# Layer norm in two token halves between the last output tiles and the next weight chunks, its root on GpSimd, products pass by pass

## The reference

```python
def layer_norm(x, g, b):
    mu = jnp.mean(x, -1, keepdims=True)
    var = jnp.mean(jnp.square(x - mu), -1, keepdims=True)
    return (x - mu) * lax.rsqrt(var + LN_EPS) * g + b

x = layer_norm(ALPHA * x + 0.5 * swiglu(x, ffn1...), ln1_g, ln1_b)      # D_FF = 2816
proj = x @ w_in                                                        # 1024 -> 5792 columns
y_a = mla_branch(...)          # latent attention, 8 heads; rms_norm of two latents (384 and 256 wide)
y_b = short_conv_branch(...)   # gated causal convolution of width 3
y_c = s5_branch(...)           # grouped state space model, scan over tokens
x = layer_norm(ALPHA * x + (g0 * y_a + g1 * y_b + g2 * y_c) @ w_o, ln2_g, ln2_b)
x = layer_norm(ALPHA * x + 0.5 * swiglu(x, ffn2...), ln3_g, ln3_b)
```

## Time and profile before

| | |
|---|---|
| runs shown, median (lowest to highest) | 2890.27 us (2888.03 to 2891.69) |
| the profiled execution's own time | 2893.35 us |
| its span, first to last instruction | 2890.6 us |
| mean granted clock of PE | 0.972 of full |
| DMA | 229.27 MB, mean 79 GB/s |

### The profile page before, as it was taken

The page is one execution under the profiler, slowest core; times in us unless marked ns, Lnnn a source line. Parts: engine busy times, 40 slices in busy tenths (PEclk is TensorE's granted clock), DMA queues, the critical chain, the costliest instruction groups (busy, mean ns, idle before and its releaser), DMA issues.

```text
span 2890.6 us, 56692 instructions
## 1 busy us (share of the span) xinstructions
PE 2710.9 (94%) x22244; PEld 2628.9 (91%) x22244; DVE 1396.7 (48%) x2020; ACT 845.8 (29%) x1236; POOL 1058.6 (37%) x477
## 2 busy tenths in 40 slices
PE   7999998899999989999889999798999999999996
PEld 7999988888889989999789999798888998999995
DVE  6954154935443662121688641649344436522126
ACT  3222223135532242222242222232245222422223
POOL 4444433312234434444334444233222343344431
PEclk9999999999999999999999999899999999999998
DMA  4323323212223323232223232232122232233322
GB/s 142 95 81 92 88 76 81 70 28 59 57 70 87 99 66 92 86 92 84 70 86 88 87 93 84 64 89 63 41 52 60 73 94 88 74 93 88 88 80 73
DMA packets 458206, 229.27 MB, mean 79 GB/s; under 512 B 38112, under 2 KB 455136, under 8 KB 458048
## 3 DMA queue, kind: packets, MB, share of 16 engines
q1 hardware_dynamic: 452864, 219.98, 27.3%
q10 hardware_dynamic: 5184, 7.14, 0.9%
HBM read 222.83 MB, written 2.10 MB: 78 GB/s over the span
## 4 chain that ended last, share of the span: by engine, by line
issue 51%; PE 25%; POOL 21%; DVE 2%; POOLq 1%; ACT 0%; DMA 0%; SPq 0%; DVEq 0%; ACTq 0%
POOL w_lo L393 21%; PE ps L438 21%; PE ps L454 1%; PE ps L737 1%; PE ps L699 1%; PE ps L716 0%; DVE ln_in L1128 0%; POOLq L392 0%; PE ps L703 0%; DVE stat L1143 0%; PE ps L463 0%; DVE stat L1159 0%; DVE ln_in L1112 0%; DVE stat L1129 0%; POOLq L398 0%
## 5 line engine op out<-in xcount | busy, mean ns | idle before, releaser
L393 POOL TENSOR_TENSOR w_lo<-w_raw,w_hi 128x1024 fp32r<-128x1024 f32 (+3 forms) x472 | 1055.9, 2242 | 1785.5 <-ACT w_hi L825 1785.3
L438 PE MATMUL ps<-x_hi,w_hi 128*128 128x264 f32 x4000 | 827.8, 288 | 20.0 <-DVE ln_in L1193 10.2
L438 PE MATMUL ps<-x_lo,w_hi 128*128 128x264 f32 x4000 | 817.6, 286 | 0.0
L438 PE MATMUL ps<-x_hi,w_lo 128*128 128x264 f32 x4000 | 816.8, 286 | 0.0
L825 ACT ACTIVATE w_hi<-w_raw 128x1024 fp32r<-128x1024 f32 (+3 forms) x475 | 453.8, 959 | 867.3 <-PE ps L438 736.9
L438 PEld LDWEIGHTS ps<-x_hi,w_hi 128*128 128x128 f32 x4000 | 627.1, 189 | 32.3 <-issue 24.3
L438 PEld LDWEIGHTS ps<-x_lo,w_hi 128*128 128x128 f32 x4000 | 622.3, 189 | 0.0
L438 PEld LDWEIGHTS ps<-x_hi,w_lo 128*128 128x128 f32 x4000 | 621.6, 189 | 0.0
L1180 DVE TENSOR_TENSOR hid_rest<-hid_rest,ps 128x528 f32<-128x528 f32 x88 | 61.9, 704 | 564.3 <-PE ps L438 537.4
L438 PE MATMUL ps<-hid_hi,w_hi 128*128 128x264 f32 x1408 | 292.5, 289 | 13.4 <-DVE ln_in L1112 12.5
L438 PE MATMUL ps<-hid_lo,w_hi 128*128 128x264 f32 x1408 | 289.6, 287 | 0.0
(11 more groups left out here) (272 smaller groups left out, 3134.4 us busy)
## 6 DMA issues: line engine op xcount, KB each, us to landing
w_raw<-in_ffn_w_gate SPq DMA_DIRECT2D x91, 512.0 KB, 3.8
w_raw<-in_w_in SPq DMA_DIRECT2D x90, 512.0 KB, 3.9
w_raw<-in_ffn_w_up SPq DMA_DIRECT2D x88, 512.0 KB, 3.8
w_raw<-in_ffn_w_down SPq DMA_DIRECT2D x64, 512.0 KB, 3.9
w_raw<-in_ffn_w_down SPq DMA_DIRECT2D x32, 384.0 KB, 3.4
w_raw<-in_w_o SPq DMA_DIRECT2D x16, 512.0 KB, 3.9
w_raw<-in_conv_w_out SPq DMA_DIRECT2D x16, 256.0 KB, 2.8
w_raw<-in_s_w_out SPq DMA_DIRECT2D x16, 256.0 KB, 3.2
```

The costliest lines, as they stand in the source:

```text
L393: pool.tensor_tensor(w_lo[:, s, 0:n], w_raw[:, c % RAW, 0:n], w_hi[:, s, 0:n].bitcast(f32), ALU.subtract).then_inc(w_split, 1)
L438: ins = nc.tensor.matmul(out[0:m, h], w[:, s, cols], x[:, k0 + k, h * HALF:(h + 1) * HALF], start=first and k == 0 and n == 0, stop=last a ...
```

## The change

Feed-forward parts are 6, 8 and 8 hidden tiles. Of the last part's eight output tiles (and of the eight of `w_o`), the first four are made whole and the last four in halves: all four for the first 264 tokens, then all four for the others, each half in a PSUM bank of its own. The norm is done for each half of the tokens by itself: sums, variance, root, scaling; the first half's tail on DVE and ACT is interleaved with taking the second half's tiles. The next four chunks are rounded and split during it, and their products start with the first half: two chunks tile by tile, the second half's sums, the other two chunks, then the same for the second half. The root is a power of -0.5 on POOL, for the latents of the mixer too; ACT's square roots and DVE's reciprocals go. Provisional mean (now of two tiles) and mean stay in PSUM and are subtracted from there. ACT makes all squares. `product` runs all input tiles of one pass before the next pass, and waits for `w_lo` only ahead of the third. `z` stays from the norm for the next block, and after the mixer is rebuilt in the merge loop. In the mixer, convolution tile 2 is before the q latents. S5 table steps move by one part. The output is stored in 16 pieces instead of 8.

```diff
-PARTS = [(0, 8), (8, 8), (16, 6)]
+PARTS = [(0, 6), (6, 8), (14, 8)]
+WHOLE = KD // 2
+HALF_BANK = {4: 0, 5: 2, 6: 1, 7: 3}
 ...
+            def root(l, which, h):                                   # POOL
+                pool.wait_ge(ln_var, (l * 3 + which) * 2 + (h + 1))
+                pool.tensor_tensor(stat[:, 0, HALVES[h]], stat[:, 0, HALVES[h]],
+                                   minus_half[:].to_broadcast([P, HALF]), ALU.pow).then_inc(ln_root, 1)
+            def norm(l, which, c0):
+                root(l, which, 0)
+                for n in range(SLOTS):
+                    split(l, c0 + n)
+                root(l, which, 1)
 ...
+                for c in range(B_M1 + SLOTS, B_HEAD):
                     split(l, c)
+                    if c == B_CONV + 1:
+                        pool.wait_ge(rms_taken, l + 1)
+                        pool.tensor_tensor(stat[:, 3:5], stat[:, 3:5], minus_half[:].unsqueeze(2).to_broadcast([P, 2, L]),
+                                           ALU.pow).then_inc(rms_root, 1)
 ...
+            def product(out, c, k0, hi, lo, n_tiles, first, last, m=P, at=0, split=None, halves=(0, 1)):
+                for n, (w, x) in enumerate(((w_hi, hi), (w_hi, lo), (w_lo, hi))):
+                    if n == 2 and split is not None:
+                        split_ready(*split)
+                    for k in range(n_tiles):
+                        for h in halves:
+                            ins = nc.tensor.matmul(out[0:m, h], w[:, s, cols], x[:, k0 + k, HALVES[h]], ...)
 ...
+            def first_products(l, c, x0, n):
+                for h in range(2):
+                    for j in range(2):
+                        pe.wait_ge(z_half[1], n * 4 + (4 + 2 * h + j + 1))
+                    by_tiles(l, [pair(0), pair(1)], c, xh, xl, x_ready[h], x0, halves=(h,))
+                    if h == 0:
+                        layer_norm_sums(n, 1)
+                    for j in (2, 3):
+                        rounded(l, c + j)
+                        ins = product(pair(j), c + j, 0, xh, xl, KD, True, True, split=(l, c + j), halves=(h,))
 ...
+            def last_tiles(l, which, c, hi, lo, nk):                 # PE
+                for h in range(2):
+                    for d in range(WHOLE, KD):
+                        ...
+                        for p, (w, x) in enumerate(((w_hi, hi), (w_hi, lo), (w_lo, hi))):
+                            for k in range(nk):
+                                ins = nc.tensor.matmul(ps[:, bank, 0:HALF], w[:, s, k * P:(k + 1) * P], x[:, k, HALVES[h]], ...)
+                        ins.then_inc(half_done if h == 0 else chunk_done, 1)
+                        if h == 1 and d == WHOLE:
+                            layer_norm_sums(n, 0)
 ...
+            def layer_norm(l, which, bd):                            # ACT
+                for d in range(WHOLE):
+                    round_ahead(l, bd + d)
+                for k in range(3):
+                    square(l, which, k)
+                round_ahead(l, bd + WHOLE)
+                square(l, which, 3)
+                for k in range(4, KD):
+                    square(l, which, k, 0)
+                square(l, which, 4, 1)
+                round_ahead(l, bd + 5)
                 for k in range(KD):
+                    norm_tile(l, which, k, 0)
+                    if k in (1, 4, 6):
+                        square(l, which, {1: 5, 4: 6, 6: 7}[k], 1)
+                        round_ahead(l, bd + {1: 6, 4: 7, 6: 8}[k])
+                for k in range(KD):
+                    norm_tile(l, which, k, 1)
 ...
+                def take_half(k, h):                                 # DVE
+                    ins = stt(z[:, k, cols], ps[:, HALF_BANK[k], 0:HALF], scale, z[:, k, cols], MUL, ADD)
+                    follow(ins, z_half[h], n * 4 + (k - 3) + 4 * h)
+                    follow(tt(z[:, k, cols], z[:, k, cols], ps[:, 6 + h, 0:HALF], SUB), ln_dev, n * 12 + (1 + k + 4 * h))
+                    st.done(tt(S[:, cols], S[:, cols], z[:, k, cols], ADD))
 ...
+                def tail(h):
+                    cols = HALVES[h]
+                    mean, var = ps[:, 4 + h, 0:HALF], stat[:, 0, cols]
+                    dve.wait_ge(ln_stat, n * 5 + (5 + 2 * h))
+                    ...                                              # four dependent operations: the variance
+                    st.done(ts(mean, mean, 1.0 / D_MODEL, None, MUL))
+                    dev = lambda k: tt(z[:, k, cols], z[:, k, cols], mean, SUB)
+                    dev(0)
+                    st.done(dev(1))
+                    dve.wait_ge(ln_root, n * 2 + (h + 1))
+                    for k in range(KD + 1):
+                        if k < KD:
+                            tt(z[:, k, cols], z[:, k, cols], var, MUL).then_inc(ln_scaled, 1)
+                        if k + 2 < KD:
+                            st.done(dev(k + 2))
+                        if k:
+                            dve.wait_ge(ln_hi, m * KD + k)
+                            tt(xl[:, k - 1, cols], z[:, k - 1, cols], xhf[:, k - 1, cols], SUB).then_inc(x_ready[h], 1)
+                        if h == 0 and k in (1, 4, 6):
+                            j = {1: 5, 4: 6, 6: 7}[k]
+                            st.done(add_square(j - 1, HALVES[1], j + 4))
+                            take_half(j, 1)
+                        if h == 0 and k == 7:
+                            add_square(KD - 1, HALVES[1], 12).then_inc(ln_sums, 1)
 ...
+                conv_tile(l, 2, st)
                 latent_tiles(l, 0, st)
-                conv_tile(l, 2, st)
+                conv_tile(l, 3, st)
                 latent_tiles(l, 1, st)
-                conv_tile(l, 3, st)
```

More of the change, by code:

```diff
@@ L396, in ffn @@
             def ffn(l, b0):
-                for (f0, nf), at_ in zip(PARTS, PART_AT):
-                    with pool.Fori(0, nf // 2) as i:
+                for part, ((f0, nf), at_) in enumerate(zip(PARTS, PART_AT)):
+                    with pool.Fori(1 if part == 0 else 0, nf // 2) as i:
                         for n in range(4):
@@ new lines, in ffn, with gate @@
+            def ffn(l, b0, w):
+                def gate(part, i, j, ahead=True):
+                    (f0, nf), bu = PARTS[part], b0 + PART_AT[part]
+                    c = bu + 2 * j
+                    if ahead:
+                        round_ahead(l, c, 1, i, nf // 2)
+                    if isinstance(i, int):
+                        act.wait_ge(chunk_done, done_at(l, c + 4 * i))
+                        dst = glf[:, 2 * i + j]
+                    else:
+                        act.wait_ge(chunk_done, done_at(l, c) + i * 4)
+                        dst = glf[:, ds(i * 2 + j, 1)].rearrange("p a t -> p (a t)")
+                    ACTV(two(dst), pair(2 * j), ACT.Silu).then_inc(silu_done, 1)
+                    round_ahead(l, c + 1, 1, i, nf // 2)
+                gate(0, 0, 0, ahead=False)
@@ L953, in _ @@
                         ACTV(two(kvf[:, n - MT - 3]), src).then_inc(m1_taken, 1)
-                act.wait_ge(rms_taken, l + 1)
-                ACTV(stat[:, 3:5], stat[:, 3:5], ACT.Sqrt).then_inc(rms_sd, 1)
                 for n in range(3 * MT):
@@ L1149, in layer_norm @@
-                ins.then_inc(ln_sums, 1)
-                take(KD - 1)
-                dve.wait_ge(ln_stat, n * 3 + 2)
-                st.done(ts(two(stat[:, 0]), pair(2), 1.0 / D_MODEL, None, MUL))
-                st.done(tt(stat[:, 3], stat[:, 0], stat[:, 0], MUL))
-                dve.wait_ge(ln_stat, n * 3 + 3)
-                stt(two(stat[:, 2]), pair(3), 1.0 / D_MODEL, two(stat[:, 3]), MUL, SUB).then_inc(ln_var, 1)
-                for k in range(2):
-                    dev(k)
-                dve.wait_ge(ln_sd, n + 1)
@@ L1159, in layer_norm @@
[L1159 to L1167 removed]
+                dve.wait_ge(ln_stat, n * 5 + 3)
@@ new lines, in layer_norm @@
+                st.done(ts(pair(3), pair(2), 1.0 / (2 * P), None, MUL))
+                st.done(stt(two(S), pair(3), -2.0, two(S), MUL, ADD))
+                for k in range(3):
+                    tt(two(z[:, k]), two(z[:, k]), pair(3), SUB).then_inc(ln_dev, 1)
+                dve.wait_ge(ln_dev, n * 12 + 3)
+                st.done(tt(S, S, z[:, 2], ADD))
+                st.done(add_square(1, square=2))
+                take(3)
+                follow(tt(two(z[:, 3]), two(z[:, 3]), pair(3), SUB), ln_dev, n * 12 + 4)
@@ L1400, in latents_begin @@
                     dve.memset(v[:, 2 * L:2 * L + P].bitcast(f32), 0.0)
-                dve.wait_ge(rms_sd, l + 1)
-                for n in range(2):
-                    ins = nc.vector.reciprocal(stat[:, 3 + n], stat[:, 3 + n])
-                st.done(ins)
+                dve.wait_ge(rms_root, l + 1)
             def latent_tiles(l, n, st):
```

362 lines of the change are left out of this document (182 added, 180 removed).

## The result

The changed kernel takes 3664.95 us (median of 4 runs, 3662.66 to 3667.11), the kernel before on the same chip 2890.98. The ratio is 1.268, 95% interval 1.266 to 1.270: slower by 27%, where 2860 us was forecast. The profiled execution took 3662.66 us, its span 3660.8, the mean granted clock 0.868 (0.972 before).

What follows compares the result with a forecast made beforehand. TensorE, busy 94% of the span, bounds the kernel; only its waits and lower clock can be won. Norms 17.7, mixer 9.4 and start 3 make 30 us off, from the 2890.27 us median to 2860, range 2818 to 2916.

Steps and rivals of the forecast that it cites:

- R is not in the trace: Step pricing POOL's unseen power for 264 columns: 1.7 us from the reciprocal's 6.5 ns a column, range 0.8 to 3.9.
- R: Time of one POOL power of 264 columns in a norm half, taken as 1.7 us; 6.9 us for the latents' 1056.
- rival (c): Slower: power twice on each norm's path and before the mixer's splits; 2886 us at R = 3, 2926 at 5; chance 0.22.
- Norm, walk: Step-by-step norm timing from tile 4's first half product (T = 0): loss 18.5 + R or 17.5 + 2R per norm.
- Splits beside the tail: POOL splits meeting DVE's dense first-half tail in each norm: three charged at 2.0 us each, 6 us.
- Rival (b): POOL splits don't meet DVE in the norms as charged: about 40 us more gained, 2820 us; chance 0.08.
- Mixer: Earlier convolution tile wins 8.5 us and 1.4 of clock, against 5.2 of waits: +4.7 us a layer, +9.4.
- Feed-forward parts, "0": Parts of 6, 8, 8 with S5 tables moved by a part, where DVE has room: 0 us.
- Pass by pass, "0": Products ordered by pass, same matmuls and weight loads, no run of such half passes in the trace: 0 us.
- (a): The power is cheap, R = 0.8: norms 27.3, mixer 2 x 9.9, start 3, 50 us off, 2840 us; chance 0.18.
- (d): No change: R near 3, or norm tiles nearer 1.5 than 1.16 us from ACT-DVE hand-over; 2885 to 2893 us; chance 0.10.
- (e): The power costs 1.5 times the reciprocal's rate, R = 2.6, the mixer's 10.4 us: 2878 us; chance 0.11.

Runs made afterwards that it cites:

- run 3: Changed kernel with only the latents' root back on ACT's Sqrt and DVE's reciprocals, the norms' twelve powers staying on POOL: 3348.0 us, ratio 1.160.
- run 10: Kernel of run 7 with the four POOL splits beside each norm cut to 8 columns, those remainders left out: 2808.9 us, ratio 0.973.
- run 6: Kernel before with convolution tiles ahead of the latents and products pass by pass, whole-tile norms kept: 2849.2 us, ratio 0.987.
- run 7: Kernel of run 1 with the S5 table steps moved from beside the first part's down products, parts still 6, 8, 8: 2841.9 us, ratio 0.984.
- run 4: Kernel before with convolution tile 2 ahead of the query latents and tile 3 ahead of the key/value latents, roots unmoved: 2867.8 us, ratio 0.993.
- run 5: Kernel before with only each product's matmuls reordered pass by pass; waits, halves and parts stay: 2867.8 us, ratio 0.993.
- run 2: Changed kernel with a cheap product of constants in place of every POOL power, so the output is not the reference's: 2855.3 us, ratio 0.988.
- run 1: Changed kernel with all roots back on ACT's Sqrt and DVE's reciprocal, all else as changed: 2864.0 us, ratio 0.992.
- run 12: Kernel of run 1 with powers of several widths and exponents and a product on POOL behind the last output: 264-column powers 42.5 us each, product 0.62 us.
- run 11: Kernel of run 7 with the second to fourth splits beside each norm done by DVE between its tiles, nothing left out: 2824.9 us, ratio 0.978.

## Why the prediction was wrong

**The step that failed** is "R is not in the trace": the value of 1.7 us and the bounds of 0.8 and 3.9. The lower one held as a bound, the upper one was low by a factor of 11. It had scaled DVE's reciprocal, 4.9 times its subtraction, to POOL; on POOL the power is 42.44 / 0.62 = 68 times a product. No row of before showed anything like it, so a factor taken from another engine's dearest operation was no bound, and the range, the chances and the point of 3.3 us up to which the forecast could stand were all drawn inside it. An estimate from the Trainium skill's page "GPSIMD Engine Reference", section 3.1, was 2.6 us by its branch figure, 10 ns a column; the measured 161 ns a column are 16 times that.

**The mechanism was that of rival (c)**, down to its price of "2 us a norm for each us of R": 484 us for twelve powers (run 3). With R = 42.4 its formulas give 17.5 + 2 x 42.4 = 102.3 us for each of five norms and 119.8 for the last, 471 more than before; for the mixer some 167 us of waits a layer less 9.9, 314; start -3: 782 us, 3672. Measured were 3665. That it comes so near is in part luck, since the terms below are off by up to 22 us, in both directions.

**Norm, walk.** Right to some 0.5 us at the marks of the first norm: variance at T = 18.0 (18.1), DVE on its way at 466.8 (466.9), second power at T = 89.4 (variance at 46.5 + R = 88.9), last tile at T = 141.9 (141.6). Splits beside the tail: charged 2.0 us each, measured 33 us in six norms, 5.5 a norm for three (run 10). Rival (b), which had them at nothing, is out. The 264-column operations are 0.35 and 0.46 us apart as taken.

**Halves, net.** With a root of 2.4 us the formulas give the norms 9 and the start 3 us; the expectation of run 6 said 17 and 3. Measured, from run 6 to run 7: 7 us. Right in sign, too small in size. The waits of 7.5 us behind the moved S5 parameters (run 7), which run 6's kernel lacks, are inside this 7; without them it would be some 14, by an estimate.

**Mixer.** The order of convolution tiles was worth about the 2 x 9.9 us (run 4: 20, with the reciprocals still in their place). The wide power was to cost 5.2 us a layer and cost 159 (317 / 2, run 3); it held DVE's second scan, as said, though only for its first half.

**Feed-forward parts, "0": wrong**, +22 us (run 7). The steps were charged against DVE's busy share of 48%, a mean of the span. What decides is one take interval: 0.7 + 5.3 us of DVE against a product that had just become 4.4 us. DVE was busy 37.98 of 40 us in that very stretch of before (run 7's first row), so it had no room to give. The parameters, moved behind the first hidden tile, cost the 7.5 us more of that run's waits.

**Pass by pass, "0": wrong**, -18 us (run 5). Same matmuls and loads, but another order among them has another pitch. That this zero and the last nearly cancel is luck.

**Rivals.** (a) R = 0.8 is nearly run 2 (0.62 us): 2855 measured for 2840. The two wrong zeros, +22 and -18, and some 7 for the parameters account for 11 of the 15 us, if they hold in that kernel as in the others, which was not tried; the rest stays open. (d) and (e) fall with R.

With ACT's Sqrt and DVE's reciprocal in the power's place the change is a gain of 24 us (run 1), and of 44 with the tables moved (run 7). That root takes 3.1 us from the end of the variance to the end of the reciprocal (run 7, 412.94 to 416.02), in part beside other work of DVE.

## What to carry to other kernels

An operation that no row shows has no upper bound from rows of another engine. Where it sits twice on the path, work out the price per us first, as rival (c) did, and then measure the operation alone before the change is built on it; run 12 would have done. An edit charged at nothing because "the engine has room" needs the row of that very stretch and the interval between two instructions that others wait for, not the busy share of the span. Beside a dense DVE stretch, a POOL split of 2.5 us cost DVE 1.8 us on the path (run 10); the same subtraction on DVE itself, 1.2 us, was the cheaper one (run 11).

## What the runs showed of the hardware that was not expected

- POOL's elementwise power takes 160 ns a column plus 0.3 us, for exponents -0.5 and 2.0, for 32 and for 128 partitions alike (run 12). The product takes 0.62 us for 264 columns with its inputs here, 2.4 ns a column, and 4.05 us for 1056 (run 2), beside DVE's scan.
- A power on POOL holds some DVE operations and lets others by. In the mixer the first scan, which starts before the power, takes 2.36 us; the second is held until 683.3, half way through the power of 2 x 528 columns, and the scaling of `conv_u` (L1438) until its end; between them, with the power running, operations of 264 columns with two SBUF inputs take their usual 0.43 us, and those with one input in PSUM 0.70. A POOL subtraction instead holds a two-input operation to its end (2.56 us at 464.32). What decides in the power's case was not tried.
- The order of the matmuls in a product, pass by pass, makes the pitch 0.1211 instead of 0.1226 us. Why was not tried: whether the repeated use of one moving tile or of one accumulation address is the reason stays open.
